# Second layer's modulation computed inside the first layer's sample stage, with a reordered head and an earlier square of the second tile

## The reference, cut to what matters

```python
mod = jax.nn.silu(c) @ lp["w_mod"] + lp["b_mod"]          # (9, 1024) @ (1024, 3072)
shift_m, scale_m, gate_m = jnp.split(mod, 3, axis=-1)
h = rmsnorm(x, lp["norm_pre"]) * (1.0 + scale_m[:, None]) + shift_m[:, None]
proj = h @ lp["w_in"]                                      # (.., 1024) @ (1024, 2880)
# three head groups on proj: banded attention, RWKV-7 delta rule, RG-LRU; each times a silu gate
y = jnp.concatenate([ya, yb, yc], axis=-1) @ lp["w_out"]   # (.., 1024) @ (1024, 1024)
x = x + gate_m[:, None] * rmsnorm(y, lp["norm_post"])
```

## Time and profile before

| | us |
|---|---|
| median of 3 runs | 2907.37 (2906.48 to 2909.62) |
| profiled execution: its own time | 2903.72 |
| its span, first to last instruction | 2901.9 |
| PE busy | 2757.8 (95%) |
| DVE, ACT, POOL busy | 1720.0, 1338.5, 255.2 |

### The profile page before, as it was taken

The page is one execution under the profiler, slowest core; times in us unless marked ns, Lnnn a source line. Parts: engine busy times, 40 slices in busy tenths (PEclk is TensorE's granted clock), DMA queues, the critical chain, the costliest instruction groups (busy, mean ns, idle before and its releaser), DMA issues.

```text
span 2901.9 us, 63519 instructions
## 1 busy us (share of the span) xinstructions
PE 2757.8 (95%) x25044; PEld 2016.0 (69%) x25044; DVE 1720.0 (59%) x4641; ACT 1338.5 (46%) x3128; POOL 255.2 (9%) x357
## 2 busy tenths in 40 slices
PE   6999999999999999997769999999999999999976
PEld 5777777777777777775457777777777777777753
DVE  1666666666666666665416666665666666666654
ACT  1545444544554444443215544445445554444432
POOL 0010111101101011100001000111011100011000
PEclk8999999999999999999769999999999999999997
DMA  9200000000000000000660000000000000000001
GB/s 341 97 16 24 23 24 23 9 24 24 24 24 17 23 24 23 16 9 22 206 243 16 19 22 23 24 23 17 16 24 24 24 20 21 24 23 16 16 19 33
DMA packets 55176, 119.18 MB, mean 41 GB/s; under 512 B 15312, under 2 KB 27216, under 8 KB 54608
## 3 DMA queue, kind: packets, MB, share of 16 engines
q1 hardware_dynamic: 52912, 114.28, 11.5%
q10 hardware_dynamic: 1952, 0.48, 0.1%
HBM read 96.34 MB, written 18.41 MB: 40 GB/s over the span
## 4 chain that ended last, share of the span: by engine, by line
PE 91%; DVE 4%; DMA 2%; issue 1%; ACT 1%; SPq 0%; POOL 0%; DVEq 0%; POOLq 0%; ACTq 0%
PE G L468 17%; PE G L576 16%; PE M L792 15%; PE G L463 8%; PE M L463 5%; PE M L625 5%; PE M L459 4%; PE M L638 3%; PE G L693 2%; PE G L474 2%; DMA RB<-in_w_mod 2%; PE M L604 1%; PE M L674 1%; PE G L459 1%; DVE Q L1441 1%
## 5 line engine op out<-in xcount | busy, mean ns | idle before, releaser
L468 PEld LDWEIGHTS G<-hT,w_in 128*128 128x128 f32 x4224 | 495.2, 194 | 21.9 <-issue 16.5
L468 PE MATMUL G<-hT,w_in 128*128 128x128 f32 x4224 | 507.1, 278 | 3.3 <-issue 3.3
L576 PE MATMUL G<-hT,w_in 128*128 128x256 f32 (+1 forms) x2048 | 497.1, 385 | 0.0
L792 PE MATMUL M<-w_out,yT 128*128 128x512 f32 x1024 | 452.8, 596 | 5.8 <-DVE yT L1579 5.8
L576 PEld LDWEIGHTS G<-hT,w_in 128*128 128x128 f32 x2048 | 360.4, 189 | 64.7 <-issue 12.3
L792 PEld LDWEIGHTS M<-w_out,yT 128*128 128x128 f32 x1024 | 193.4, 191 | 225.2 <-issue 223.7
L463 PE MATMUL G<-w_in,hT 128*128 128x512 f32 x512 | 244.4, 610 | 0.0
L1441 DVE TENSOR_TENSOR Q<-Q,M 64x256 f32<-64x256 f32 x320 | 133.8, 418 | 130.5 <-PE M L638 127.3
L625 PEld LDWEIGHTS M<-W 64*64 64x64 f32 x4608 | 147.7, 135 | 24.3 <-issue 24.3
L625 PE MATMUL M<-W 64*64 64x64 f32 x4608 | 162.7, 219 | 0.0
L1231 POOL TENSOR_TENSOR RA<-RA,small 128x1024 f32<-128x1024 f32 x32 | 60.6, 1895 | 1136.9 <-DVE small L1493 1136.9
(11 more groups left out here) (413 smaller groups left out, 4562.7 us busy)
## 6 DMA issues: line engine op xcount, KB each, us to landing
w_in<-in_w_in SPq DMA_DIRECT2D x8, 2048.0 KB, 15.1
RA<-in_w_mod SPq DMA_DIRECT2D x16, 512.0 KB, 6.9
W<-in_w_mod SPq DMA_DIRECT2D x16, 512.0 KB, 6.9
xa<-in_x_prompt SPq DMA_DIRECT2D x16, 512.0 KB, 3.7
w_out<-in_w_out SPq DMA_DIRECT2D x2, 4096.0 KB, 18.4
G<-in_x_prompt SPq DMA_DIRECT2D x16, 512.0 KB, 3.5
x_mid<-RA SPq DMA_DIRECT2D x16, 512.0 KB, 2.9
xa<-x_mid SPq DMA_DIRECT2D x16, 512.0 KB, 3.6
```

Of the source, the lines that this page charges most:

```text
L468: last = mm(out[0:width, :], Win[:, k, col:col + width], H[:, k, :], start=k == 0, stop=k == KC - 1)
L576: last = mm(out, Win[:, k, col:col + P], moving, start=k == 0, stop=k == KC - 1)
L792: last = mm(o[:, :], yT[:, k, :], Wout[:, k, 512 * h:512 * h + 512], start=k == 0, stop=k == KC - 1)
```

## The change

- The LRU constants of both layers (`spc`, `prm` with a layer axis) are made in the first head; the constants' DMAs `reset`, `mst`, `ms`, `mit` go from SP to ACT's queue, and DVE's wait for `prm` covers all 13 DMAs of ACT.
- SP issues `cT` first, then five pieces of `w_mod`, then the rest of the constants.
- The second layer's 24 pieces of `w_mod` come into four buffers that are idle in the first sample stage (`wnext`: `KB`, two halves of `hT`, `xr`), from the last tile's end on. PE multiplies and folds them inside the sample stage (`mod_group`, `mod_fold`), ACT copies rows and folded results (`mod_row`, `mod_copy`).
- x(16), the second layer's first tile, is loaded, squared, scaled and transposed in the same stage. The second layer has no head of its own before `fill_rk`.
- `x_square(1)` (and x(17)) stands right behind `copy_rk`; the C_GB channels stand ahead of `front`; ACT's copy of them stands ahead of `decays`.
- The state stores after a layer's last tile go from SP's queue to ACT's.

```diff
@@ SP
+                def load_next(*qs):
+                    for q in qs:
+                        if q == 0:
+                            sp.wait_ge(s["y_mm"], DONE(NT - 1))
+                        elif q < 3:
+                            sp.wait_ge(s["gbc_mm"], DONE(NT - 1))
+                        elif q == 3:
+                            sp.wait_ge(s["o_ready"], DONE(NT - 1))
+                        else:
+                            sp.wait_ge(L["mod_mm"], 24 + (q - 4 + 1))
+                        sp.dma_start(wnext[q % 4], d["w_mod"][1, q]).then_inc(wmod_in[q % 4], 16)
...
+                    load_next(0, 1, 2)
+                    sp.wait_ge(s["o_ready"], DONE(NT - 1))
+                    sp.dma_start(rows(dst, NT - 1), ob).then_inc(L["y_out"], 16)
+                    load_next(3)
...
                 sp.wait_ge(L["y_out"], (l + 1) * NT * 16 + 16)
                 for buf, x in ((dcst, d["dcst"]), (dshift, d["shift_s"][l]), (dconv, d["conv_s"][l]), (dh0, d["h_s"][l])):
                     sp.dma_start(buf, x).then_inc(smp["in_small"], 16)
+                if l == 0:
+                    load_next(4, 5, 6, 7)
+                sp.dma_start(dS, d["wkv_s"][l]).then_inc(smp["kv_in"], 16)
+                if l == 0:
+                    load_next(8, 9, 10, 11)
...
+                if l == 0:
+                    load_next(*range(12, 24))
                 if l < DEPTH - 1:
 
                     sp.wait_ge(smp["pe"], AT("proj_mm", l))
                     load_w_in(l + 1)
...
+                if l < DEPTH - 1:
+
+                    sp.wait_ge(smp["dve"], AT("y", l))
+                    sp.dma_start(xa[:, :], d["x_mid"][0:P, :]).then_inc(L["x_in"], 16)
+                    load_rope(0, (l + 1) * NT)
@@ ACT
-                x_square(l * NT, hT[:, :, 1, :])
-                act.wait_ge(L["mod_out"], l + 1)
-                act.wait_ge(L["zeros"], l + 1)
-                h_lo(l * NT, hT[:, :, 0, :])
-                h_hi(l * NT, hT[:, :, 0, :])
-                for step in (copy_rk, copy_wka, copy_v, low_rank, decays):
+                if l == 0:
+                    x_square(0, hT[:, :, 1, :])
+                    act.wait_ge(L["mod_out"], 1)
+                    act.wait_ge(L["zeros"], 1)
+                    h_lo(0, hT[:, :, 0, :])
+                    h_hi(0, hT[:, :, 0, :])
+                copy_rk(l * NT)
+                x_square(l * NT + 1, hT[:, :, 1, :])
+                for step in (copy_wka, copy_v, low_rank):
                     step(l * NT)
-                x_square(l * NT + 1, hT[:, :, 1, :])
                 act.wait_ge(L["g0_mm"], l + 1)
                 A(stBC[:, 0], G0[:, :].rearrange("p (c t) -> p c t", c=4), ACT.Copy).then_inc(L["g0_out"], 1)
+                decays(l * NT)
@@ DVE
+            cleared(0)
+            dve.wait_ge(L["prm"], 32 + 128 + 48)
+            for l in range(DEPTH):
+                lam = par(l, "lam")
...
+            for l in range(DEPTH):
+                if l == 0:
+                    x_mean(0)
+                    for g in range(MODG):
+                        dve.wait_ge(L["mod_mm"], 4 * (g + 1))
+                        cp(rowbuf[g % 2], (G0, G1)[g % 2][:, :]).then_inc(L["row_out"], 1)
...
+                if mixed:
+                    x_mean((l + 1) * NT)
                 for h in range(2):
                     dve.wait_ge(L["row_mm"], l * (ROWS - MODG) + (len(DGROUPS) + h + 1))
-                    cp(rowbuf[h], (G0, G1)[h][:, :]).then_inc(L["row_out"], 1)
+                    cp(srow[h], (G0, G1)[h][:, :]).then_inc(L["row_out"], 1)
```

More of the change, by code:

```diff
@@ L500, in _, with mod_group @@
-                mod_channels(MODG - 1).then_inc(L["modT_mm"], 1)
+                    return to_channels(rowbuf[g % 2], g, M0, 1 + B, [(P * j, P, 9 * (4 * g + j)) for j in range(4)])
+                def mod_group(g):
+                    if g > 3:
+                        pe.wait_ge(L["mfold_out"], g if g == 5 else 1)
+                    for j in range(4):
+                        q = 4 * g + j
+                        pe.wait_ge(wmod_in[q % 4], 64 + (q // 4 + 1) * 16)
+                        column_groups(MB[g][:, P * j:P * j + P], cpad, lambda k: wnext[q % 4][:, k, :])\
+                            .then_inc(L["mod_mm"], 1)
@@ new lines, in mod_fold @@
+                def mod_fold(g):
+                    pe.wait_ge(L["mrow_out"], g + 1)
+                    for j in range(4):
+                        last = mm(MB[g][:, 9 * j:9 * j + 9], mrow[:, P * j:P * j + P], fold[:, 0:1 + B], start=True, stop=True)
+                    last.then_inc(L["modT_mm"], 1)
+                if l == 0:
+                    pe.wait_ge(L["padded"], 1)
+                    pe.wait_ge(L["layer_end"], 1)
+                    for q in range(24):
+                        pe.wait_ge(wmod_in[q % NWM], (q // NWM + 1) * 16)
+                        g, j = q // 4, q % 4
+                        if q == 4:
+                            pe.wait_ge(L["const"], 32)
+                        column_groups((G0, G1)[g % 2][:, P * j:P * j + P], cpad, lambda k: wmod[q % NWM][:, k, :])\
+                            .then_inc(L["mod_mm"], 1)
+                        if j == 3 and g > 0:
+                            mod_channels(g - 1)
+                    mod_channels(MODG - 1).then_inc(L["modT_mm"], 1)
@@ L901, in _ @@
                 for h in range(2):
-                    last = to_channels(h, MODG + len(DGROUPS) + h, M3, B, [(P * j, P, B * (4 * h + j)) for j in range(4)])
+                    last = to_channels(srow[h], MODG + l * (ROWS - MODG) + len(DGROUPS) + h, M3, B, [(P * j, P, B * (4 * h + j)) for j in range(4)])
                 last.then_inc(smp["pe"], 1)
+                if mixed:
+                    x_lo((l + 1) * NT)
                 pe.wait_ge(smp["dve"], AT("osq", l))
@@ L1183, in _ @@
                 for c in range(2):
-                    A(dth[:, c, :], dgr[:, c, :], ACT.Tanh, scale=spc[:, 9, c:c + 1])
-                    last = A(daa[:, c, :], dgr[:, c, :], ACT.Exp, scale=spc[:, 9, c:c + 1])
+                    A(dth[:, c, :], dgr[:, c, :], ACT.Tanh, scale=spc[:, l, 9, c:c + 1])
+                    last = A(daa[:, c, :], dgr[:, c, :], ACT.Exp, scale=spc[:, l, 9, c:c + 1])
                 last.then_inc(smp["act"], 1)
+                if mixed:
+                    load_small(l + 1)
+                    for g in range(4, MODG):
+                        mod_row(g)
+                        mod_copy(g)
                 act.wait_ge(smp["dve"], AT("lru_t", l))
@@ L1293, in _, with x_mean, modulation @@
                 dve.wait_ge(L["zeros"], l + 1)
-                dve.wait_ge(L["prm"], (l + 1) * 144)
-                lam = par("lam")
-                ll(ts(spc[:, 10, :], lam, -1.0, None, ALU.mult))
-                tt(spc[:, 0, :], lam, spc[:, 10, :], ALU.max).then_inc(L["sp1"], 1)
+            def x_mean(m):
+                dve.wait_ge(s["x_root"], DONE(m))
+                ts(xa[:, :], xa[:, :], small[:, 7:8], ROOT_D, ALU.mult, ALU.mult).then_inc(s["xn_ready"], 1)
+            def modulation(l):
+                ll(tt(mod[:, :, :], (modr[:, :, :] if l else M0[:, 0:216].rearrange("p (q b) -> p q b", q=24)),
+                      over(par(l, "bmod"), 2, 9), ALU.add))
+                ll(ts(gs[:, :, :], mod[:, 8:16, :], 1.0, None, ALU.add))
+                tt(gs[:, :, :], gs[:, :, :], over(par(l, "npre"), 2, 9), ALU.mult).then_inc(L["mod_out"], 1)
@@ L1299, in _ @@
+            cleared(0)
+            dve.wait_ge(L["prm"], 32 + 128 + 48)
+            for l in range(DEPTH):
+                lam = par(l, "lam")
+                ll(ts(spc[:, l, 10, :], lam, -1.0, None, ALU.mult))
+                tt(spc[:, l, 0, :], lam, spc[:, l, 10, :], ALU.max).then_inc(L["sp1"], 1)
                 dve.wait_ge(L["sp2"], 2 * l + 1)
-                ll(ts(spc[:, 2, :], spc[:, 1, :], 1.0, None, ALU.add))
-                ll(ts(spc[:, 3, :], spc[:, 2, :], -1.0, None, ALU.add))
```

321 lines of the change are left out of this document (189 added, 132 removed).

## The result

The changed kernel takes 2920.93 us in the median of five runs (2919.39 to 2922.37), beside 2907.37 for the kernel before in the same session: 1.0046 times as long, 95% interval 1.0031 to 1.006. It is slower. The forecast was 2902, range 2889 to 2915.

The account below looks back on a forecast made before the run. PE was 95% busy, so it read waits leaving PE: first head (DMA-bound), layer change, last sample stage. First head +18.6, layer change -22.3, second head -1.7 sum to -5.4: 2898.3, plus 3.7 for the median, 2902.0; range 2889 to 2915.

Parts of the forecast that it names:

- steps (2), (3) and (6): First head: small DMAs land at 20; two spc chains put first row at 30.7; early x(1) square stalls ACT to 90.7.
- step (2): First head: ACT's 13 small DMAs, behind at most six w_mod pieces (8 us), land at 20.
- rival A's early landing: First head: ACT's small DMAs do not wait behind SP's stream; head costs 10.6 us, time 2894; chance 0.15.
- step (4): First head: 16 pieces and six folds remain, 12 us slow, then eight pieces quick; modulation done at 51.
- The last term: First head: the work from x(1)'s landing at 90.7 to x_hi at 113.9 takes 23.2 us.
- Step (1): Layer change: w_mod's flow begins at 1388.4, piece 15 lands at 1408.3, so proj_mm ends 18.5 us later.
- Step (3): Layer change: the fold behind sa_mm waits for mod_row(4), behind eight load_small issues on ACT; +6.1 us.
- Step (4): Layer change: fold ahead of s_mm +1.3 us, modulation(1) in DVE's chain +0.95; mod_group(5), 4.3 us, fits in 5 us.
- Step (5): Layer change: x(16) lands at 1470.2, scaled at 1473.2, ahead of DVE's second row copy at 1473.8; costs nothing.
- step (6): Layer change: o_mm ends at 1475.6 and fill_rk starts at 1481.9 instead of 1504.2, -22.3 us.
- Rival C: Layer change: x(16), behind w_in and five stores on SP, lands 12 us later; time 2914; chance 0.2.
- keeps its chain: Last sample stage: chain unchanged, as ACT's six state stores (4.6 us) end just ahead of the square root.

Follow-up runs that it names:

- e1: Changed kernel with layer 0's square and scaling of x(1) put back behind decays and operands: 2906.8 us, ratio 1.0 to the kernel before.
- e2: Kernel before with only layer 0's square and scaling of x(1) moved early: 2923.71 us, ratio 1.0059.
- e4: Changed kernel with DVE's wait for the small DMAs and two scale chains behind the fourth and fifth row copies: 2909.49 us, ratio 1.0008.
- e10: Changed kernel with ACT's state stores behind the first four groups' copies and DVE's clearing ahead of scaling x(16): 2912.69 us, ratio 1.0016.
- the nine kernels above: Kernels leaving the state stores in place, with the same program up to there: the projection ends 46.6 to 49.5 us behind the store.
- e6: Changed kernel with ACT's eight issues of layer 1's small weights behind its square root of the variance: 2921.3 us, ratio 1.0053.
- e9: Changed kernel with x(16) and its rope loaded ahead of the last of w_in's eight pieces on SP: 2914.49 us, ratio 1.0027.
- e5: Changed kernel with ACT's state stores behind its last square root and DVE's clearing ahead of scaling x(16): 2923.18 us, ratio 1.0055.
- e12: Changed kernel with the edits of e1, e3, e4, e9, e10 and e6 together: 2878.41 us, ratio 0.9901 to the kernel before.
- e14: e12 with DVE's scaling of x(16) put behind the output's squares: 2874.33 us, ratio 0.9893 to the kernel before.
- e11: Changed kernel with the edits of e1, e3, e4 and e9 together: 2883.59 us, ratio 0.9922 to the kernel before.
- e3: Changed kernel with the load of w_out behind that of x(1) on SP's queue: 2912.41 us, ratio 1.0023 to the kernel before.
- e13: e12 with x(16) loaded behind the fifth of w_in's pieces instead of the seventh: 2871.41 us, ratio 0.9878 to the kernel before.
- e7: Changed kernel with DVE's scaling of x(16) behind the output projection's row copies and squares: 2918.05 us, ratio 1.0042 to the kernel before.

## Why the prediction was wrong

**The first head** (+27.2 to the first store, +24.3 to `x_hi`, forecast +18.6). The mechanism of steps (2), (3) and (6) was right, and e1, e2 and e4 show it. Mis-sized: step (2) put the small DMAs' landing at 20, it was 22.9 (rival A's early landing did not come; the last section tells why); step (4) let PE run at the quick pace from the ninth piece on, so that the modulation ended at 51 (its own terms add up to 51.6); it ended at 59.35, 3 us of it from the late first row and the rest from folds at 1.88 and pieces at 1.08, the slow values, again from 46.9 on. So x(1) landed at 97.4 and not at 90.7. The last term, 23.2 from landing to `x_hi`, was 22.2. Behind `x_hi` another 2.9 us were lost, for which the forecast had no term: 2.4 of them because PE, which had stood 4.9 us ahead of `x_hi`, had a granted clock of 0.50 from 119.6 to 124.0, where it was 1.00 before. The forecast had the step that costs and gave it too little, because it summed PE's pace as if the gap that it predicted itself would not slow PE again.

**The layer change** (`fill_rk` -10.7 against -22.3). Step (1), "so the flow begins at 1388.4 and piece 15 is there at 1408.3": +18.5 against +24.5. It had counted the state stores as 4.5 us more of DMA time in a flow without gaps. They cost 7.3 by the two executions of the changed kernel and e10 (4.5 to 7.3 against the range of the nine kernels above), nearly all of it PE's wait for piece 3 and the low clock right behind it. The other 3.1 us of the miss are not theirs: e10 still ends the projection 17.1 us later than the kernel before, where the step's sum without its 4.5 us gives 14.0. The pieces come in turns through four buffers and not in one flow, and PE waits 2.8 us for pieces of the third and fourth turn in e10. Step (3), the fold behind eight issues: forecast 6.1 and less than 1 for `mod_group(4)`, together measured 3.8, 3.7 of it the issues (e6). Step (4): `modulation(1)` 0.95, measured 0.9. Step (5), "So it just costs nothing", is the step that failed. The output projection starts 29.7 us later than before, against 26.9 forecast; from there to `fill_rk` it takes 22.0 us, where step (6) has 13.2, and these 8.8 are the larger part of the 11.6 missed. x(16) was there for ACT 102.9 us behind the store, DVE held the output's row copies for it, and from the output projection to `fill_rk` lay 9.5 us too many (e9). Its arithmetic had x(16) land at 93.8 behind the store, and missed by 9.1 us: 5.8 because `w_in` was issued at 60.0 and not 54.2 (the late projection), and the rest behind it: SP needed from 1490.5 to 1498.3 to issue the stores ahead of x(16), 4.4 us of it for one of 4 KB, which looks like a full ring, though no view shows the ring's state. Rival C named this mechanism and its price (12 us); I gave it 0.2 as if it stood against the forecast alone, while it comes on top of the late projection.

**The second head** brought 4.1 us instead of 1.7, counted to `x_hi`, of which 2.6 are left at the first store; the early square costs nothing there, as x(17) has landed when ACT comes to it: its square follows `copy_rk` without a wait, as forecast.

**The last sample stage**, "keeps its chain: ACT's six state stores end just ahead of the square root", is wrong. In the changed kernel's timeline of ACT:

```profile
2842.21 1.20 ACTq L1248 DMA_DIRECT2D out_h_p<-hcar  x1
2843.44 1.28 ACT L1265 ACT_TABLE_LOAD   x1 [8.61 <-issue]
2844.73 0.21 ACT L1265 ACTIVATE stA<-stA 128x8 f32<-128x8 f32 x1
```

The stores do end when the square root is wanted, but the load of its table, done early before, is queued behind them: +0.9, of which 0.5 is left at the output projection. The Trainium skill, ScalarE: Activation LUTs, What ACT_TABLE_LOAD costs, gives some 1283 ns for one, and the trace agrees (1.28). The other 3.0 us are PE's clock, not a wait: the output projection's 32 products took 6.57 us at a granted clock of 0.55 and the last sum 3.31 at 0.55, against 4.95 at 0.73 and 1.95 at 1.00 in the kernel before (1.00 is the level of 2.4 GHz, 0.50 that of 1.2). With the stores moved (e5, e10, e12 to e14) the end takes 78.2 to 78.6; with the stores in place it took 81.6 to 81.9 in six kernels and 78.9 in three (e6, e9, e11). So between executions at the same pace the stores' place makes 0.3 to 0.7 us. Why the slow pace comes in six of nine is open; none of the seven kernels without ACT's stores there has it (the kernel before, e2, e5, e10, e12 to e14), so the stores may bring it on, which no run shows.

**The size of the whole**: forecast -5.4 on the span's stretches, measured +18.7: head 8.6, layer change 10.6, end 3.5 and tiles 1.4 on the unfavourable side. None of the rivals gave a time above 2914, since each was worked out as if the forecast's other terms held. By the rivals' own splits the chances of same and slower add up to 0.35 and 0.18, not 0.34 and 0.19.

## What to carry to other kernels

An instruction that waits for a load blocks everything behind it on its engine, so moving it earlier needs the load's landing time first, and the load's place in the queue is the cheaper thing to move (e3, e9, e13). When a chain is shortened, redo the landing times of everything behind the stream that it starts; x(16) was late again in e6 and e12 for that reason. Here six small stores cost least where little else was in flight (e10), not where their engine was idle. A load's time on the chain of waits is not yet a stall: read beside it how long the engine itself stood (6.5 of 9.5 us, and 0.5 of 11.4).

## What the runs showed of the hardware beyond that

A full stream on one queue holds small stores on the other for long: e5's `h_p`, 1 KB on ACT's queue, took 22.0 us to land while SP's `w_in` ran at some 366 GB/s at first (1478 to 1490), `shift_p` (3.5 KB) 17.3. The first two of the six, 64 KB each, still landed in 5.5 and 5.9. Issued before that stream (e13), the same six took 1.6 to 9.8. In e5 from 1488 to 1492 both queues move as many packets, and 232 GB/s in all:

```profile
q1 hardware_dynamic: 464, 0.93, 105.2%
q10 hardware_dynamic: 464, 0.00, 6.5%
```

The next two stretches of 4 us have 168 and 169, then 378 and 379, at 84 and 210 GB/s. The Trainium skill, DMA: Bandwidth & Descriptors, Queues, rings and completion order, says that an engine round-robins between the rows it has work for, and these counts agree with that. `h_p` is the last of its queue's 1,760 packets, so by that rule it waits until those ahead of it have had their turns. The same shows where the prediction read the wait of the earlier trace rows as a sign against this rule: from 1462 to 1466 in the kernel before SP's queue moves 445 packets and ACT's 443, and in the changed kernel's first head 542 and 543 from 8 to 12, 380 and 379 from 16 to 20. ACT's 13 small DMAs are late because they are some 1,700 packets that take turns with SP's larger ones. The same section says that a semaphore's increment waits for earlier writes of its engine, which may add to the wait; no run separates the two.

The six stores, 0.2 MB in 1,760 packets, slow what SP has in flight beside and behind them: from 1410 to 1415 the changed kernel moves 39 GB/s, e10 without them 345. The same page, Specifications, puts the smallest size at line rate at 512 B. When ACT's queue was alone in e10 (1442 to 1445), 793 of its 921 packets were below it, and it moved 24 GB/s.

PE's pace within the same stretch is not fixed by the program. The 16 products of the projection's third and fifth groups, in the timelines of e12 and then of e13, whose programs are the same up to there:

```profile
1398.00 2.39 PE L503 MATMUL G<-w_in,Q 128*32 128x512 f32 x16
1409.95 1.92 PE L503 MATMUL G<-w_in,Q 128*32 128x512 f32 x16
```

```profile
1400.40 3.64 PE L503 MATMUL G<-w_in,Q 128*32 128x512 f32 x16
1416.30 3.64 PE L503 MATMUL G<-w_in,Q 128*32 128x512 f32 x16
```

The granted clock over these rows was 0.77 (1397.8 to 1400.4) and 1.00 (1409.95 to 1414.5) in e12, and 0.50 in both places in e13 (0.50 is the level of 1.2 GHz). Ahead of the first row PE had stood 1.0 us for pieces of `w_mod` in e12 and 2.2 in e13; whether that decides it is not shown. In e13's execution the projection took 8.4 us more than in e12's, that run lasted 2879.6 us, and the other three of e13 2870.1 to 2872.1. Stages with gaps can thus differ by 8 us between runs of one kernel. That may be why e7 and e9 have runs 15 us apart; only one execution of each was profiled. Single stretches of profiled executions are to be trusted only where several kernels agree.
